# The delta rule's inverse in two half chains, a combined small projection, and later decay tables and transposes

## The reference

```python
gcum = jnp.cumsum(gi, axis=1)
decay = jnp.exp(jnp.where(causal, gh[..., :, None] - gh[..., None, :], -jnp.inf))
a_low = jnp.einsum('bihd,bjhd->bhij', kb, ki) * decay * strict
sol = lax.linalg.triangular_solve(a_low + eye, rhs, left_side=True, lower=True)
u, w = sol[..., :GDN_DV], sol[..., GDN_DV:]
v_new = u - jnp.einsum('bhcd,bhdv->bhcv', w, S)
S = S * jnp.exp(glast)[:, :, None, None] + jnp.einsum('bjhd,bhjv->bhdv', kdec, v_new)
```

## Time and profile before

| | |
|---|---|
| median of three runs | 2277.09 us |
| profiled execution | 2267.16 us |
| its span | 2265.3 us |
| PE busy | 2179.1 us, 96% |
| DVE busy | 1339.4 us, 59% |
| ACT busy | 878.5 us, 39% |
| POOL busy | 499.7 us, 22% |
| mean granted clock of PE | 0.99 |

### The profile page before, as it was taken

One profiled execution on the slowest core, in us unless ns is written; L12 is line 12 of the kernel. 1 busy time (PEld: TensorE's weight loads), 2 busy tenths in 40 slices (PEclk: granted clock), 3 DMA queues, 4 the chain that ended last, 5 costly groups with the idle time before them and its releaser, 6 DMA issues.

```text
span 2265.3 us, 38624 instructions
## 1 busy us (share of the span) xinstructions
PE 2179.1 (96%) x15412; PEld 1975.5 (87%) x15412; DVE 1339.4 (59%) x2436; ACT 878.5 (39%) x1759; POOL 499.7 (22%) x432
## 2 busy tenths in 40 slices
PE   7999989999999999999999999999999999999996
PEld 6887878999898798999988788889998888899996
DVE  5677567545476657523566776763456777555324
ACT  5444257323333317411343433663334333463101
POOL 3433324331010002100233333333210101021001
PEclk9999999999999999999999999999999999999998
DMA  6654456677463334455466444557676533444433
GB/s 232 230 191 154 158 176 207 226 258 261 155 243 121 112 114 148 165 170 183 165 222 240 175 162 165 202 184 254 227 246 199 204 112 112 140 144 155 168 122 149
DMA packets 98193, 410.84 MB, mean 181 GB/s; under 512 B 11168, under 2 KB 12256, under 8 KB 84192
## 3 DMA queue, kind: packets, MB, share of 16 engines
q1 hardware_dynamic: 97440, 407.98, 51.3%
q10 hardware_dynamic: 576, 0.40, 0.1%
HBM read 257.17 MB, written 151.16 MB: 180 GB/s over the span
## 4 chain that ended last, share of the span: by engine, by line
PE 82%; DVE 9%; issue 4%; ACT 3%; POOL 1%; DMA 0%; ACTq 0%; DVEq 0%; POOLq 0%
PE ps L1161 78%; PE ps L1164 4%; DVE wk L1630 2%; DVE wk L1644 1%; POOL w_low L2150 1%; DVE wk L1605 0%; DMA row<-in_rows 0%; DVE wk L1609 0%; DVE wk L1608 0%; DVE et L1566 0%; ACT w_hi L1878 0%; DVE wo_parts L1724 0%; POOL rs L2108 0%; DVE gss L1579 0%; DVE acc L1816 0%
## 5 line engine op out<-in xcount | busy, mean ns | idle before, releaser
L1161 PE MATMUL ps<-w_hi,hT_hi 128*128 128x256 f32 x1792 | 527.5, 294 | 3.2 <-DVE hT_lo L1480 3.2
L1161 PE MATMUL ps<-w_low,hT_hi 128*128 128x256 f32 x1792 | 508.5, 284 | 0.0
L1161 PE MATMUL ps<-w_hi,hT_lo 128*128 128x256 f32 x1792 | 502.8, 281 | 0.0
L2150 POOL TENSOR_TENSOR w_low<-w_loaded,w_hi 128x512 fp32r<-128x512 f32 x208 | 287.9, 1404 | 412.2 <-ACT w_hi L1878 412.1
L1161 PEld LDWEIGHTS ps<-wk 128*128 128x128 f32 x2336 | 296.8, 192 | 91.1 <-DVE wk L1630 22.5
L1161 PE MATMUL ps<-wk 128*128 128x128 f32 (+2 forms) x2336 | 344.7, 287 | 21.0 <-DVE wk L1657 5.3
L1161 PEld LDWEIGHTS ps<-w_low,hT_hi 128*128 128x128 f32 x1792 | 343.6, 192 | 2.8 <-issue 2.4
L1161 PEld LDWEIGHTS ps<-w_hi,hT_hi 128*128 128x128 f32 x1792 | 338.8, 189 | 6.6 <-DVE hT_lo L1480 3.8
L1161 PEld LDWEIGHTS ps<-w_hi,hT_lo 128*128 128x128 f32 x1792 | 342.6, 191 | 0.0
L1161 PE MATMUL ps<-hT_hi,w_hi 128*128 128x512 f32 x768 | 330.3, 430 | 7.2 <-POOL w_low L2150 4.9
L1161 PE MATMUL ps<-hT_lo,w_hi 128*128 128x512 f32 x768 | 303.4, 395 | 0.0
(11 more groups left out here) (197 smaller groups left out, 3183.4 us busy)
## 6 DMA issues: line engine op xcount, KB each, us to landing
w_loaded<-in_w_in SPq DMA_DIRECT2D x104, 512.0 KB, 5.0
w_split<-w_hi SPq DMA_DIRECT2D x52, 1024.0 KB, 6.9
w_split<-w_low SPq DMA_DIRECT2D x52, 1024.0 KB, 9.4
w_hi<-w_split SPq DMA_DIRECT2D x104, 512.0 KB, 6.3
w_low<-w_split SPq DMA_DIRECT2D x104, 512.0 KB, 7.2
wo_loaded<-in_w_out SPq DMA_DIRECT2D x32, 512.0 KB, 4.2
wk<-cum_rows SPq DMA_DIRECT2D x32, 512.0 KB, 4.4
wo_split<-wo_hi SPq DMA_DIRECT2D x32, 512.0 KB, 8.0
```

Of the source, the lines that this page charges most:

```text
L1161: return nc.tensor.matmul(o, a, b, start=start, stop=stop)
L2150: tt(w_lo[at], wr[at], w_hi[at], ALU.subtract)\
```

## The change

- The four chunks of the inverse become two halves of two chunks each: every `gdn_p` and `gdn_xx` step, with its waits, banks and DVE instructions, is there twice with half the columns, in the order p of half 0, p of half 1, xx of half 0, xx of half 1.
- The table of the next head, `gdn_decay`, moves from ahead of the inverse to behind the first chunk of the state chain.
- In the small projection high and low weights lie side by side (48 columns), so that one product with hT_hi gives both; 16 products for 24. The sum of the two rows is made in the turning, by four products with a stack of two identities.
- The third and fourth x tile's transposes go behind slices 3 and 7 of the first half piece in all parts.
- The constants of the rows have a semaphore of their own.
- The planner: `NEAR` 40 for 120, `OUT_WAIT` 3500 for 2500; in the last part the last `KEEP` = 4 output steps of the group before the last are kept until the front is out, and are then emitted only at waits of `HOLD` = 500 ns or more, or when no mixing step is left; the last group's output steps go by token half first; the last weights' loads stand behind the kept steps in SP's order. Its costs are those of the halves.

The diff, cut to its core:

```diff
 def mixing_steps(p):
-        out += [("gdn_turn", p, h), ("gdn_gram", p, h), ("gdn_x0", p, h)] + [("gdn_decay", p, h + 1)] * (h + 1 < GH)
+        out += [("gdn_turn", p, h), ("gdn_gram", p, h), ("gdn_x0", p, h)]
         for k in range(1, LEVELS):
-            out += [("gdn_p", p, h, k), ("gdn_xx", p, h, k)]
+            out += [(name, p, h, k, j) for name in ("gdn_p", "gdn_xx") for j in range(2)]
         for c in range(NT):
             out += [("gdn_s", p, h, c), ("gdn_v", p, h, c), ("gdn_o", p, h, c)]
+            out += [("gdn_decay", p, h + 1)] * (c == 0 and h + 1 < GH)
...
-                if p and (i, half) == (0, 0):
-                    add(("norm", p, 2), ("rescale", p, 2), *needs)
...
-                    if not p and (i, half) == (0, 0) and q in (3, 7):
-                        add(("norm", 0, 2 + q // 4), ("rescale", 0, 2 + q // 4))
-                    if p and (i, half, q) == (0, 0, 1):
-                        add(("norm", p, 3), ("rescale", p, 3))
+                    if (i, half) == (0, 0) and q in (3, 7):
+                        add(("norm", p, 2 + q // 4), ("rescale", p, 2 + q // 4))
...
         if step[0] == "mix_turn":
-            outs.extend(("out", *step[1:3], u, tp) for u in range(UNITS) for tp in range(NT // 2))
+            if step[1:3] == (PARTS - 1, GROUPS - 1):
+                outs.extend(("out", *step[1:3], u, tp) for tp in range(NT // 2) for u in range(UNITS))
+            else:
+                outs.extend(("out", *step[1:3], u, tp) for u in range(UNITS) for tp in range(NT // 2))
...
+        if unit and unit[1:3] == (PARTS - 1, GROUPS - 2):
+            if front_at < len(front) and not stuck and len(outs) <= KEEP or front_at == len(front) and step and wait < HOLD:
+                unit = None
...
-OUT_WAIT = 2500
+OUT_WAIT = 3500
-NEAR = 120
+KEEP = 4
+HOLD = 500
+NEAR = 40
...
-            loads.append((where["proj", PARTS - 1, len(PIECES) - 1, 1, Q - 1], u, ("tail", PARTS - 1, u)))
+            loads.append((max(where["proj", PARTS - 1, len(PIECES) - 1, 1, Q - 1], where["out", PARTS - 1, GROUPS - 2, UNITS - 1, 0]),
+                          u, ("tail", PARTS - 1, u)))
...
                 elif k == "small":
                     for kk in range(KD):
-                        mm(b, hi[:, kk, :], hT_hi[:, kk, :], kk == 0, False)
-                        mm(b, lo[:, kk, :], hT_hi[:, kk, :], False, False)
-                        i = mm(b, hi[:, kk, :], hT_lo[:, kk, :], False, kk == KD - 1)
+                        if kk:
+                            mm(b[0:NSM, :], both[:, kk - 1, 0], hT_lo[:, kk - 1, :], False, False)
+                        if kk == KD - 1:
+                            mm(b[0:NSM, :], both[:, kk, 0], hT_lo[:, kk, :], False, False)
+                        i = mm(b[0:2 * NSM, :], both[:, kk].rearrange("p e n -> p (e n)"), hT_hi[:, kk, :], kk == 0, kk == KD - 1)
                 elif k == "small_turn":
-                        i = nc.tensor.transpose(b[:, t * NSM:(t + 1) * NSM], smT[:, t * P:(t + 1) * P], ident[0:NSM, 0:NSM])
+                        i = mm(b[:, t * NSM:(t + 1) * NSM], smT[:, t * P:(t + 1) * P], con[0:2 * NSM, C_TWO:C_LEV])
...
                 elif k == "gdn_p":
-                        wait_emptied(pe, ("gdn_xx", p, h, lv - 1))
+                        wait_emptied(pe, ("gdn_xx", p, h, lv - 1, j))
-                    for c in range(NT):
-                        i = mm(b[:, c * P:(c + 1) * P], aT[:, c, :], X[:, c, :])
+                    for c in range(2):
+                        i = mm(b[:, c * P:(c + 1) * P], aT[:, 2 * j + c, :], X[:, 2 * j + c, :])
...
                 elif k == "gdn_xx":
-                        empty(tt(X, X, bank4(s), ALU.subtract), s)
+                        empty(tt(X[:, own], X[:, own], bank4(s)[:, 0:2], ALU.subtract), s)
...
                 elif k == "gdn_p":
-                        nc.vector.transpose(XT.rearrange("p c n -> p (c n)"), X.rearrange("p c n -> p (c n)")).then_inc(S["gdn_turned"], 1)
+                        nc.vector.transpose(XT[:, own].rearrange("p c n -> p (c n)"), X[:, own].rearrange("p c n -> p (c n)")).then_inc(S["gdn_turned"], 1)
-                    empty(tt(PP, bank4(s), over_rows(mask), ALU.mult), s)
+                    empty(tt(PP[:, own], bank4(s)[:, 0:2], over_rows(mask, 2), ALU.mult), s)
...
-                act.dma_start(row[:, l, :], rows[l].partition_broadcast(P)).then_inc(pars_in, 16)
+                act.dma_start(row[:, l, :], rows[l].partition_broadcast(P)).then_inc(rows_in, 16)
```

More of the change, by code:

```diff
@@ L61 @@
 C_ZERO = C_PW2 + 8
-C_LEV = C_ZERO + 4
+C_TWO = C_ZERO + 4
+C_LEV = C_TWO + NSM
 C_DM = C_LEV + LEVELS * 128
@@ L94, in constants @@
     c[:, C_LEV:C_LEV + P] *= -1.0
+    c[:2 * NSM, C_TWO:C_LEV] = np.tile(np.eye(NSM), (2, 1))
     c[:, C_PW:C_PW + 8] = -0.5
@@ L336, in play @@
         elif k == "small":
[L337 removed]
+            mark("n", pe(16 * 233))
             mark(("small", p), act(590, "n"))
@@ L410, in play @@
             mark("n", both(700, "a"))
-            mark(("xt", p, r[0], 1), both(640, "n"))
-            mark(("x", p, r[0], 1), dve(600))
+            mark("n", both(640, "n"))
+            mark("n", dve(600))
+            for j in range(2):
+                at["xt", p, r[0], 1, j] = at["x", p, r[0], 1, j] = at["n"]
             mark(("kq", p, r[0]), pool(1400))
@@ L417, in play @@
         elif k == "gdn_p":
-            h, lv = r
+            h, lv, j = r
             if 1 < lv < LEVELS - 1:
-                mark(("xt", p, h, lv), dve(600, *after))
-            mark("n", pe(4 * LINE))
-            mark(("pp", p, h, lv), dve(640, "n"))
+                mark(("xt", *step[1:]), dve(370, *after))
+            mark("n", pe(2 * LINE))
+            mark(("pp", *step[1:]), dve(380, "n"))
             if lv == LEVELS - 1:
                 after = []
-                mark("n", pe(4 * TURN))
-                mark(("xt", p, h, lv), act(560, "n"))
+                mark("n", pe(2 * TURN))
+                mark(("xt", *step[1:]), act(340, "n"))
         elif k == "gdn_xx":
-            h, lv = r
-            mark("n", pe(4 * LINE))
-            mark(("x", p, h, lv + 1) if lv < LEVELS - 1 else ("xt", p, h, LEVELS), dve(640, "n"))
+            h, lv, j = r
+            mark("n", pe(2 * LINE))
+            mark(("x", p, h, lv + 1, j) if lv < LEVELS - 1 else ("xt", p, h, LEVELS, j), dve(380, "n"))
         elif k == "gdn_s":
@@ L577, in known @@
                 "split_out": lambda: ("small2", p) if r == (0, 0) else None,
-                "gdn_p": lambda: ("gdn_fin1", p, r[0] - 1) if r[1] == 1 and r[0] else None,
+                "gdn_p": lambda: ("gdn_fin1", p, r[0] - 1) if r[1:] == (1, 0) and r[0] else None,
                 "gdn_fin1": lambda: ("proj", p, AT["gz", r[0] // 2], 1, Q - 1),
@@ L880, in hybrid_kernel @@
         last_in = [sem(f"x_last_loaded{i}") for i in range(NT)]
-        pars_in, later = sem("pars_loaded"), sem("later_consts_loaded")
+        pars_in, rows_in, later = sem("pars_loaded"), sem("rows_loaded"), sem("later_consts_loaded")
         xf_in = sem("xf_loaded")
@@ L1144, in wsm_parts @@
             r, n = unit_no["small", p] % 2, KD * NSM
-            return wo[:, r, 0:n], wo_parts[:, r, 0:n], wo_parts[:, r, n:2 * n]
+            both = wo_parts[:, r, n:3 * n].rearrange("p (k e n) -> p k e n", k=KD, e=2)
+            return wo[:, r, 0:n].rearrange("p (k n) -> p k n", k=KD), both
         @block.tensor
@@ L1282, in _ @@
                 elif k == "gdn_p":
-                    h, lv = s[2], s[3]
+                    h, lv, j = s[2:]
                     if lv == 1:
@@ L1624, in _ @@
                 elif k == "gdn_xx":
-                    h, lv = s[2], s[3]
+                    h, lv, j = s[2:]
+                    own = slice(2 * j, 2 * j + 2)
                     wait_filled(dve, s)
@@ L1900, in _ @@
                     loaded_unit(act, ("small", p))
-                    w, _, hi = wsm_parts(p)
-                    A(hi, w, ACT.Copy).then_inc(S["wsm_hi_ready"], 1)
+                    w, both = wsm_parts(p)
+                    A(both[:, :, 0], w, ACT.Copy).then_inc(S["wsm_hi_ready"], 1)
                 elif k == "small2":
@@ L1979, in _ @@
                     wait_filled(act, tag)
-                    empty(A(XT, bank4(tag), ACT.Copy), tag)
+                    empty(A(XT[:, 2 * s[4]:2 * s[4] + 2], bank4(tag)[:, 0:2], ACT.Copy), tag)
                 elif k == "gdn_s" and not no_state(s):
@@ L2153, in _ @@
                     pool.wait_ge(S["wsm_hi_ready"], p + 1)
-                    w, lo, hi = wsm_parts(p)
-                    tt(lo, w, hi, ALU.subtract).then_inc(S["wsm_lo_ready"], 1)
+                    w, both = wsm_parts(p)
+                    tt(both[:, :, 1], w, both[:, :, 0], ALU.subtract).then_inc(S["wsm_lo_ready"], 1)
 def kernel(**inputs):
```

50 lines of the change are left out of this document (25 added, 25 removed).

## The result

The changed kernel takes 2201.38 us (median of 4 runs, 2199.89 to 2202.74), the kernel before 2275.88 us in the same comparison (4 runs). The ratio is 0.9675 [0.9659, 0.9692], 74.5 us less. The forecast was 2235 with a range down to 2211: the direction was right, the size was not. The gain was to be 41.8 us and is 1.8 times that.

The account below looks back on a forecast made before the run. The prediction took PE, 2179.1 us of a 2265.3 us span, to bound the kernel. Its terms summed to -41.8 us on a median of 2277.1, giving 2235 us, with an 80% range of 2211 to 2263.

Parts of the forecast that it names:

- Half chains, the waits themselves: In the inverse: PE's short waits for DVE shrink with halved steps; -2 us taken, bounds -29 and +48.
- Rival 3: In the chains: DVE becomes the pace through added work, +19 us, 2296; chance 0.09.
- Bare chunks: State chain: slices left by a shorter inverse fill eight chunks with nothing beside them; -8 us, bounds -13 and 0.
- Gate stops: Last DeltaNet head's gate: eight left-over slices would cover two PE stops; -9 us, bounds -14.5 and +3.
- rival 2: Whole kernel: stops only move to the next gate; small projection, start, x and end win -19.8 us, 2257; chance 0.24.
- Weight stops: PE's stop for split output weights, as the first SSD group begins earlier; -3 us, bounds -11.8 and +4.
- Small projection: Small projection: 16 products per part for 24, saving 7.4 us less dearer turning; -5.3 us.
- Start: Kernel start: own semaphore for the rows lets DVE begin earlier; -1 us, bounds 0 and -1.7.
- Later transposes: Parts 1 to 3: moved x transposes remove x stops, DVE late next; -5.5 us, bounds -6.9 and +2.4.
- The end: Last part: kept output steps fill waits and finals run beside PE; -8 us, bounds -9.1 and +6.
- Two slices a level: Sign in the inverse's chains: two filling slices a level, with DVE near 85%.
- rival 1: Whole kernel: all stops go, -65 us, 2212; chance 0.17.

Follow-up runs that it names:

- e4: Kernel before, shifted 96 bytes, with half chains alone and old thresholds: 2240.29 us, ratio to before 0.9845.
- e6: Changed kernel with whole chains and both old planner thresholds (NEAR 120, OUT_WAIT 2500): 2240.61 us, ratio to before 0.9848.
- e5: Changed kernel with the old near threshold (NEAR 120 for 40): 2216.72 us, ratio to before 0.9743.
- e9: Kernel before, shifted 96 bytes, with whole chains and only the later decay table: 2252.90 us, ratio to before 0.9911.
- e7: Changed kernel with the next head's decay table back ahead of the inverse: 2234.29 us, ratio to before 0.9821.
- e10: Kernel before, shifted 96 bytes, with half chains and later decay table together, old thresholds: 2238.91 us, ratio to before 0.9844.
- e1: Kernel before with 96 unused bytes behind the constants, plan untouched: 2267.03 us, ratio to before 0.9962.
- e2: Changed kernel with 32 more unused bytes behind the constants, 128 in all: 2204.07 us, ratio to before 0.9684.
- e11: Changed kernel with the third and fourth x tile's transposes of parts 1 to 3 at their old places: 2212.89 us, ratio to before 0.9731.
- e16: Changed kernel with its end as before: no kept output steps, no token halves, old place of last loads; 2203.73 us, ratio to before 0.9696.
- e8: Changed kernel with the last part's x loads behind the last output weights in SP's order: 2196.17 us, ratio to before 0.9651.
- e14: Kernel before, shifted 96 bytes, with half chains and both new thresholds: 2235.59 us, ratio to before 0.9830.
- e3: Changed kernel with whole chains, new thresholds and all else kept: 2284.09 us, ratio to before 1.0037.

## Why the prediction was wrong, step by step

**The step that failed** is "Half chains, the waits themselves": "With DVE this full I take little: -2". Its lower bound, -29, is what the trace shows: waits in the inverse fell from 40 to 10 us (the count over all records finds 40 before, where the prediction had 29). The bound was worked out from rows, and so was the condition: two halves and a slice are 1.61 us of PE work, a half is ready after 1.25. What I used to talk it away was a DVE share near 85%. The share came out near the forecast, 87%, and at that share PE hardly waits. That the chain could shrink to 32.9 us without filling DVE has a reason that the prediction left out: a shorter chain holds fewer slices, and so fewer conv steps. In that chain there are 12 of them with 13.1 us where there were 18 with 18.8, and DVE's work fell from 33.5 us to 28.7, though the chain's own instructions cost more. The row price was right per instruction: 128x256 masks take 404 ns where 128x512 took 684, 124 ns a pair:

```profile
L1658 DVE TENSOR_TENSOR wk<-ps,con 128x256 f32<-128x256 f32 x192 | 76.3, 404 | 25.0 <-PE ps L1172 23.2
```

The four groups of the chain took 176.9 us and take 210.9, +34 where I had 39. The durations of all DVE instructions add up to 38.6 us more, but DVE is only 20 us busier, since instructions that follow each other overlap by some 0.08 us at their ends (two of 0.42 us start 0.34 apart), and there are 256 more of them. The rule of the Trainium skill (VectorE: DVE Perf Modes, "The TRN2 errata") on tiling at 512 or more holds in this trace as a price per instruction, 124 ns a pair. It doesn't decide the time: e4 wins 26.7 us with the halves and e6 loses 39 without them and their thresholds, since DVE isn't the bound. Rival 3 (DVE the pace) fell with it: it had the chain shrink and DVE's work in it stay.

**No term at all** for two things. The near threshold was folded into the halves as "puts a slice there"; e5 prices it at 15. The later decay table was named only as making the chain end earlier; e9 gives it 14 with whole chains, e7 33 in the end, e10 1.4 in between. It can't be said which part of that is its own. What the early place costs is ACT's wait for it, with weight splits queued behind (e7).

**A cause not foreseen**: 24 new constant columns move every buffer behind them. By e1 the kernel before gains 9.4 us from that alone; by e2 it is 2.7 in the changed one, within the noise.

**Bare chunks**, -8 (eight chunks): three or so are left near 176 and 1249, of before's eight. Right in kind. But the ones at 1249 now lead to the longest stretch of low clock, here with the 4 us in front of it:

```profile
1249.40:1253.20 3.80, 2.28 (x12) 1.61 (x12) 2.34 (x9) 2.84 (x5) 1.94 (x2) 1.00 0.56 130
1253.20:1266.90 13.70, 12.21 (x48) 10.47 (x48) 5.51 (x17) 2.06 (x5) 0.51 (x1) 0.50 0.56 214
```

It follows the chain with 54 slices, which left none for the chunks behind it. No stop there is over 1 us; PE worked 2.28 of 3.80 us before the clock fell.

**Gate stops**, -9: the stop at 289.7 is 4.4 us, at 1373.5 4.4, where they were 5.5 each. Windows of the first, answering to the earlier trace rows:

```profile
286.00:289.60 3.60, 3.60 (x17) 2.92 (x16) 3.53 (x8) 3.51 (x9) 0.67 (x1) 1.00 0.40 113
289.60:294.10 4.50, 0.52 (x3) 0.09 (x1) 4.32 (x4) 4.47 (x11) 4.14 (x4) 1.00 0.59 191
```

I had said that eight slices would cover it. Six stand there now, where one did, so five times 0.7 us, 3.5, did arrive. But the stop is only 1.1 shorter, for the gate comes later. The DVE timeline of before, from the last drain to the gate:

```profile
304.83 0.69 DVE L1742 TENSOR_TENSOR wk<-ps,con 128x512 f32<-128x512 f32 x1 [1.20 <-PE ps L1161]
...
311.02 1.49 DVE L1695 TENSOR_TENSOR gate<-gate,ss 128x512 f32<-128x512 f32 x1
```

and the same of after:

```profile
284.24 0.69 DVE L1756 TENSOR_TENSOR wk<-ps,con 128x512 f32<-128x512 f32 x1 [1.20 <-PE ps L1172]
...
289.08 2.58 DVE L1539 SCALAR_TENSOR_TENSOR slot<-raw,par,slot 128x512 f32<-128x512 f32 x2
...
292.80 1.50 DVE L1709 TENSOR_TENSOR gate<-gate,ss 128x512 f32<-128x512 f32 x1
```

7.7 us from 304.83 to the gate's end at 312.51, and 10.1 from 284.24 to 294.30: the slices that should cover the gate bring two conv steps, 2.58 us, in front of it in DVE's queue. 3.5 us of cover less 2.4 of delay is the 1.1 measured. The stop stays as rival 2 had it, by what rival 3 had named for the chains: conv steps in DVE's queue ahead of what PE waits for. In e4 and e5, with the old near threshold, PE's rows have no wait for this gate, so it could be covered; e5 has 3.7 us for a split weight near that place instead (at 304.6).

**Weight stops**, -3: not bought. Two more came that before has not, 2.1 us at 897.17 and 1.3 at 1985.38, both in the row "issue" and before an output step in parts 1 and 3; SP issues loads of split output weights at 891.62, so they look like late loads too, which no run tests. 3.69 us at 348.6 and 3.79 at 1433.1 stand, and this is the window behind the first, at a clock of 0.57:

```profile
352.50:356.00 3.50, 3.50 (x19) 3.50 (x19) 2.09 (x4) 3.47 (x11) 0.00 (x0) 0.57 0.73 242
```

**Small projection**, -5.3: right, 7.6 less 2.6. **Start**, -1: the stop before the first slice is 1.56 us where it was 3.08, so -1.5, inside its bounds. **Later transposes**, -5.5: e11 prices them at 11.5, but in a plan where the old place costs 10.0 us of stops, against 5.5 in before. Seen from before, 5.5 us of x stops went and 4.5 (1.2 and 3.3) came behind ACT's queue. "What is late next is DVE" was false: ACT was.

**The end**, -8: 2.3 by e16. Finals do run beside PE; these are the first and the last that answer to the earlier trace rows:

```profile
2184.01 1.28 DVE L1830 SCALAR_TENSOR_TENSOR acc<-acc,frs,post 128x1024 f32<-128x1024 f32 x1
...
2192.32 1.28 DVE L1830 SCALAR_TENSOR_TENSOR acc<-acc,frs,post 128x1024 f32<-128x1024 f32 x1 [2.12 <-POOL frs L2159]
...
2196.63 1.22 DVE L1835 TENSOR_TENSOR acc<-acc,wk 128x1024 f32<-128x1024 f32 x1
```

Two pairs run from 2184.01 beside output steps, two behind. From the last drain's end at 2190.2 to the last final's at 2197.9 it is 7.7 us, as forecast. But the loads of the last weights, named in the prediction with +6 and then given 1.1, took 5.3 us; e8 returns 5.2.

**The sum over the misses.** Chain, chunks, gates and weights were -22 together. e6 has 39 for halves and thresholds, with the later table already in both. The misses upward (chains, table, placement) outweigh those downward (gates, weights, end). Part of the distance is the base: I added 9.9 us to carry the traced sum to the median, and the traced execution of after lies 1.4 above its own median. Against the traced executions the forecast was 2225.4 and 2202.7 came, 22.7 off; against the medians 34.

**The signs named beforehand.** PE waits for the last weights: this sign of being wrong came true. The gate stops are a fifth shorter and DVE is not over 95% in the chains. "Two slices a level" came in two of the sixteen chains; the others hold 14 to 54 in their six levels. The low-clock stretches are as many as before (ten for nine, the one at the end counted in both), which was to speak for rival 2, yet the time lies below even rival 1's 2212: neither rival had the table's or the placement's share.

What is not settled: the split of the 74.5 us between halves, threshold and later table, since they aren't additive (e10, e14), and why the buffers' place sets the pace of the products. The small projection and the start were read from the traces and not run by themselves.

## What to carry to other kernels

When a bound worked out from rows says that a wait goes, and the only thing against it is the busy share of an engine that isn't the bound, work out what share is left in the shorter stretch, with the work that leaves it, before you give the bound up; here it stayed at 87%. Look at which queue a step blocks, and not only at its own length. When cover is moved in front of a wait, count what it puts into the queue that the wait is for. Price scheduling edits together, and where a planner has thresholds, compare with those that suit each form: e3 alone would have said 83 us for the halves, e6 says 39.

## What the hardware showed that was not expected

The distance between products depends on where their operands lie: a wide slice of three takes 0.700 us with the buffers shifted by 0 or 128 bytes, and also in the changed kernel moved to 128, and 0.690 at 96. Narrow slices take 0.720 at the old place and 0.707 at the others, an output step 2.847 and 2.820 to 2.826. The granted clock fell to 0.50 for 13.7 us at 1253.2 behind no stop over 1 us, PE having worked 2.28 of the 3.80 us before. An idle engine isn't the only thing behind a "wait for issue": here it was a queue whose head waited 9.63 us for a DMA.
